# A float32 mixture of 32 experts beside a context stream: fewer turns, every second one of three experts

## What is computed

```python
def routed_moe(h, w_router, b_router, w1, b1, w2, b2):     # h: 256 tokens x 1024, 32 experts
    logits = (xt @ w_router + b_router).astype(jnp.float32)
    top_v, top_e = lax.top_k(logits, 4)
    gates = jax.nn.softmax(top_v, axis=-1)
    ...
    def expert_block(args):                                # w1[e]: 1024 x 2048, w2[e]: 1024 x 1024
        xb, e = args
        return clamped_swiglu(xb @ w1[e] + b1[e]) @ w2[e] + b2[e]
    ...
    y = jnp.zeros((T, D), h.dtype).at[row_tok].add(yb * row_gate[:, None].astype(yb.dtype))

# second block, first layer, for the context rows: retention, then a squared-ReLU MLP
yc = finish(o_cf + flip(o_cb), g_c)
ctx = layer_norm(DN_ALPHA * ctx + g1c * yc, ln_g[i, 0], ln_b[i, 0])
ctx = layer_norm(DN_ALPHA * ctx + g2c * sq_relu_mlp(hc, mlp_w1[i], mlp_w2[i]), ln_g[i, 1], ln_b[i, 1])
```

## Time and profile before

| | before |
|---|---|
| median of 3 runs | 2652.26 us (2649.83 to 2655.31) |
| profiled execution | 2649.32 us, span 2647.5 us |
| TensorE busy | 2388.3 us (90% of the span) |
| VectorE / ScalarE / POOL busy | 55% / 24% / 4% |
| moved by DMA | 711.89 MB, mean 269 GB/s |
| granted TensorE clock, mean | 0.967 of full |

### The profile page before, as it was taken

The page is one execution under the profiler, slowest core; times in us unless marked ns, Lnnn a source line. Parts: engine busy times, 40 slices in busy tenths (PEclk is TensorE's granted clock), DMA queues, the critical chain, the costliest instruction groups (busy, mean ns, idle before and its releaser), DMA issues.

```text
span 2647.5 us, 43597 instructions
## 1 busy us (share of the span) xinstructions
PE 2388.3 (90%) x18084; PEld 1596.5 (60%) x18084; DVE 1448.4 (55%) x2805; ACT 633.9 (24%) x795; POOL 111.1 (4%) x195
## 2 busy tenths in 40 slices
PE   6998988999999899888889898899998999996998
PEld 5887633444444453345445454477767987774897
DVE  2446445444343343555444444576668766776876
ACT  1111211122121121111111111133443433332432
POOL 0000010000000000000000000000000000000000
PEclk8999999999999999999999999999999999998999
DMA  8788888988999799888989888543435542322652
GB/s 345 297 309 328 325 349 328 363 351 349 390 361 368 301 376 373 346 309 324 364 311 365 324 351 319 220 167 139 155 127 207 190 143 98 110 98 88 221 185 77
DMA packets 111249, 711.89 MB, mean 269 GB/s; under 512 B 12480, under 2 KB 13136, under 8 KB 36128
## 3 DMA queue, kind: packets, MB, share of 16 engines
q1 hardware_dynamic: 85904, 616.93, 60.1%
q0 software_dynamic: 25168, 92.38, 9.8%
HBM read 705.06 MB, written 4.19 MB: 268 GB/s over the span
## 4 chain that ended last, share of the span: by engine, by line
PE 74%; DVE 19%; issue 3%; ACT 3%; DMA 1%; DVEq 0%; SPq 0%; ACTq 0%
PE bank L269 25%; PE bank L2176 6%; PE bank L2157 5%; PE bank L1894 5%; PE bank L1932 4%; PE bank L1909 3%; PE bank L1559 3%; PE bank L1416 2%; PE bank L2042 2%; DMA ring<-in_units_a 1%; PE bank L2261 1%; PE bank L1818 1%; PE bank L2031 1%; PE bank L2073 1%; DVE scratch L2938 1%
## 5 line engine op out<-in xcount | busy, mean ns | idle before, releaser
L269 PE MATMUL bank<-hid,scratch 128*32 128x512 f32 x816 | 339.3, 595 | 0.0
L269 PE MATMUL bank<-hT,scratch 128*32 128x512 f32 x784 | 336.3, 597 | 0.0
L1188 ACT CAST chi<-craw 128x1024 fp32r<-128x1024 f32 x128 | 133.3, 1043 | 581.2 <-PE bank L1894 172.4
L3158 DVE TENSOR_TENSOR clo<-craw,chi 128x1024 fp32r<-128x1024 f32 x128 | 155.6, 1221 | 41.7 <-ACT chi L1188 41.0
L269 PE MATMUL bank<-yacc,scratch 128*32 128x512 f32 x1128 | 175.1, 597 | 0.0
L269 PE MATMUL bank<-diag_gtmp,scratch 128*32 128x512 f32 x1128 | 173.2, 592 | 0.0
L269 PE MATMUL bank<-rows,scratch 128*32 128x512 f32 x1112 | 172.5, 600 | 0.0
L269 PE MATMUL bank<-cst,scratch 128*32 128x512 f32 x1112 | 170.4, 593 | 0.0
L1894 PE MATMUL bank<-cT_hi,chi 128*128 128x256 f32 x384 | 116.6, 304 | 40.2 <-DVE crot_lo L3132 17.2
L2948 DVE TENSOR_SCALAR scratch<-bank 128x512 f32<-128x512 f32 x32 | 22.1, 692 | 217.9 <-PE bank L269 217.9
L2944 DVE TENSOR_SCALAR scratch<-bank 128x512 f32<-128x512 f32 x32 | 22.1, 692 | 210.0 <-PE bank L269 210.0
(11 more groups left out here) (664 smaller groups left out, 6045.5 us busy)
## 6 DMA issues: line engine op xcount, KB each, us to landing
hid<-in_panels_e SPq DMA_DIRECT2D x96, 1024.0 KB, 9.9
hT<-in_panels_e SPq DMA_DIRECT2D x94, 1024.0 KB, 9.8
ring<-in_units_a SPq DMA_DIRECT2D x88, 1024.0 KB, 7.3
ring<-in_panels_m SPq DMA_DIRECT2D x64, 1024.0 KB, 5.1
yacc<-in_panels_e SPq DMA_DIRECT2D x48, 1024.0 KB, 6.7
diag_gtmp<-in_panels_e SPq DMA_DIRECT2D x48, 1024.0 KB, 8.8
rows<-in_panels_e SPq DMA_DIRECT2D x47, 1024.0 KB, 7.2
cst<-in_panels_e SPq DMA_DIRECT2D x47, 1024.0 KB, 8.3
```

The lines of the kernel that those rows point to most:

```text
L269: m = self.pe.matmul(b[s:s + STRIP, :], lhs(k)[:, s:s + STRIP], v, start=(first and k == 0), stop=(k == KT - 1))
L1188: act.copy(chi[:, h % 2, :], context_raw(h)).then_inc(cx_hi, 1)
L3158: tt(context_lower(h), context_raw(h), chi[:, h % 2, :], ALU.subtract).then_inc(cx_lo, 1)
```

## The change

The 12 turns after the start turn have, in alternation, two experts (96 and 32 slots) and three (64, 32 and 32 slots). Six turns of two and six of three hold the other 30 experts, so that there are 13 turns where there were 16. By the sorting the 6 fullest experts get 96 slots, the next 6 get 64, the other 18 get 32. The order of loads becomes: for each half of a panel, one load for each expert of the turn. The eight places are handed round load by load (`place_of(m) = (m - 4) % 8`) and no longer by panel, and a load waits for the half panel that used its place eight loads before (`user_before`). SP's loop over turns is written out. TensorE's wait is for all halves of a half panel at its start. The context stream has 12 points in a turn, so one lies in the middle of each panel too; points of a turn of three get 5 shares of the pieces, points of a turn of two 2. The further turns load one panel half for both experts, and there may be 18.

```diff
-TURNS = (32 - STATIC) // 2
+SHARES = ((MANY, SLOTS - MANY), (64, 32, 32)) * 6
+TURNS = len(SHARES)
-POINTS = 6
+POINTS = 12
+HELD = 12
...
+STEPS = [(panel, h) for panel, shares in ((6 * (turn + 1) + j, shares) for turn, shares in enumerate((FIRST_SHARES,) + SHARES, -1)
+                                          for j in range(6)) for h in range(2) for _ in shares]
+def place_of(m):
+    return m if m < HELD else (m - 4) % 8
+def user_before(m):
+    return STEPS[m - 12 if m < 20 else m - 8]
...
+    share = [5 if len(SHARES[n // POINTS]) == 3 else 2 for n in range(number - 1)]
+    ends = [sum(share[:n + 1]) for n in range(number - 1)]
     for n in range(len(pieces) - 2):
-        at[n * number // (len(pieces) - 2)].append(n)
+        at[next(k for k, end in enumerate(ends) if n * ends[-1] < end * (len(pieces) - 2))].append(n)
...
+    def rows(self, b, lhs, first, h):
+        panels = self.halves(h)
+        for k in range(4 * h, 4 * h + 4):
+            for n, s in enumerate(range(0, SLOTS, STRIP)):
+                v = panels[self.owner[n]][:, k % 4, :]
                 m = self.pe.matmul(b[s:s + STRIP, :], lhs(k)[:, s:s + STRIP], v, start=(first and k == 0), stop=(k == KT - 1))
...
+            def next_half(src, m, h):
+                panel, half = user_before(m)
+                if released[half] < panel + 1:
+                    sp.wait_ge((E["half0"], E["done"])[half], panel + 1)
+                    released[half] = panel + 1
+                half_panel(src, m, h)
...
-            with turns(sp, TURNS, {loads: 6}) as i:
-                both = [sp.value_load(order_e[0:1, bass.ds(i * 2 + p, 1)], min_val=0, max_val=EXPERTS - 1) for p in range(2)]
+            for turn, shares in enumerate(SHARES):
+                who = [sp.value_load(order_e[0:1, first_of(turn) + p:first_of(turn) + p + 1], min_val=0, max_val=EXPERTS - 1)
+                       for p in range(len(shares))]
                 for j in range(6):
-                    panels_of_two([at(pe_, e * 6 + j) for e in both], loads)
+                    for h in range(2):
+                        for p, e in enumerate(who):
+                            next_half(at(pe_, e * 6 + j), load_of(turn, j, h) + p, h)
...
-                first_product(0, many)
+                first_product(0, lambda: beside(0))
...
-                beside(0)
-                first_product(1, many)
+                beside(1)
+                first_product(1, lambda: beside(2))
```

## The result

The changed kernel takes 2447.91 us in the median of 4 runs (2444.53 to 2454.49), against 2651.91 us before. The ratio is 0.9233, with an interval of 0.9209 to 0.9256: 204 us or 7.7% faster. Its profiled execution took 2445.24 us, span 2443.5.

A forecast was written before the change was run, and what follows sets the result against it. TensorE was taken to set the pace, with the loads following. From 2649.3 us, -151 for three turns, +24 and +3 for losses to loads and -6 for context waits gave 2519, stated as 2520 us, range 2475 to 2570.

The forecast's parts named there:

- the sum's 2519: Whole kernel: the profiled execution's 2649.3 us with all terms added, 2649.3 - 151 + 24 + 3 - 6.
- What set the pace before: Expert turns of the kernel before: TensorE sets the pace, its waits name only VectorE's tiles, and the loads follow.
- Three turns fewer, -151 us: Expert turns on TensorE: each turn dropped saves 50.4 us of matmuls, gather, transposes and combine, 151 us for three.
- The context's own waits, -6 us with -25 as its bound: TensorE waiting for context pieces in the turns: 6 us less, bounds 0 and 25, though proportion gave 39.
- The one wait on which I leaned, 2.7 us: Context stream before the change: a matmul at 567.78 waits 2.7 us for clo where two pieces stand together.
- The clock, taken as no gain: TensorE in the turns: half-speed stretches after waits; one more per turn of three would cost 10 us, inside the 24.
- The loss of turns of three, +24 and +3 us: Expert turns: TensorE and full DMA engines sharing eight places lose 4 us a turn of three, 0.5 a turn of two.
- TensorE stays alone and the context waits shrink: Rival for the expert turns: no loss to loads, 25 us of waits gone, 2476 us; chance 15%.
- the ceiling of 363 GB/s: Rival for the loads: DMA engines can't hold 407 GB/s for long; 363 as limit gives 2595 us; chance 5%.
- The rival was to decide at 19.5 us: Landing time of panel loads: 19.5 us as usual value decides; at 21 us the kernel takes 2705 us; chance 3%.
- The signs: Trace of the turns: alternately near 77 and 117 us, 1160 to 1175 together, tens of us of panel waits, DMA share 0.97.
- the second rival: Expert turns: TensorE never waits for a panel and context waits shrink by 25 us, 2476 us; chance 15%.

The follow-up runs named there:

- e3: Changed kernel with every panel load after the start turn moving half its bytes, same TensorE instructions: 2436.83 us.
- e1: Changed kernel's 12 turns, but context pieces only at the six points a turn of the kernel before: 2545.55 us, ratio 0.9606 to before.
- e2: Finer context points alone: 15 turns of two experts as before, all else as in the changed kernel: 2535.79 us, ratio 0.9556 to before.
- e8: Changed kernel with the second context piece of a point moved two depths into the following half panel on TensorE: 2436.74 us.
- e5: Changed kernel with equal shares of context pieces for every turn instead of 5 to 2: 2475.31 us.
- e6: Changed kernel with six places for half panels instead of eight: 2494.90 us.
- e13: The changed kernel itself again, five executions on one chip as reference: 2447.13 us, ratio 0.9222 to before.

## Why the prediction was right or wrong

The prediction had the right bound and the right main term, and missed by 72 us, above all because it sized the second half of the change at almost nothing. From the sum's 2519 to the profiled execution's 2445 it is 74 us: 45 are the context's waits, 20.5 the waits for panels, 11 TensorE's busy time with the gather, and 3 us outside the turns go the other way.

**What set the pace before: right.** TensorE did, and it still does (e3). One reading was loose: TensorE's list before is not VectorE's alone, 0.7 us in it is for a tile of ScalarE.

**Three turns fewer, -151 us: right in size.** e1 against before gives 143.7 us of busy time and 2.8 of the gather's wait less, at 14 us more of lost clock in the turns. The changed kernel against e2 gives 144.1 and 4.3 less, at 15 more. So a turn costs 49 us as it stands; I had 50.4. At full clock it would be 53 to 55, an estimate that still holds the cuts that go with a turn: the context stands at 146 places in e2 and at 114 in the changed kernel, at 90 before and at 72 in e1.

**The context's own waits, -6 us with -25 as its bound: this is the step that failed.** Measured are 103.6 - 52.4 = 51 us. The count of second pieces, 56 before and 32 after, was in the prediction with its proportional result of 39 us, and was then talked down: the cover between pieces would be a half panel instead of a whole one, and time won on TensorE would be lost to the loads. Neither discount held (the second comes true only one step further on, in e8). e2 has half a panel between single pieces and 9.7 us of waits, so there 3.6 us of cover is nearly always enough. Divided evenly, the waits are 1.9 us a second piece before, 1.4 in e1, 1.6 in the changed kernel. But they are not all of this kind: with the 12 new turns, 3 second pieces (e5) leave 22.4 us, and from there to the 74 of e1 each adds about 1.1 us. From e2 to before it is 1.7. The one wait on which I leaned, 2.7 us, was a short one. Here is the longest of the changed kernel, in order of time:

```profile
692.45 1.04 PE L1984 MATMUL bank<-cst,cg 128*128 128x128 f32 x8
699.78 0.80 PE L1992 MATMUL bank<-chi,crot_hi 128*128 128x512 f32 x1 [6.29 <-DVE crot_lo L3192]
700.38 0.63 PE L1992 MATMUL bank<-clo,crot_hi 128*128 128x512 f32 x1
700.80 0.63 PE L1992 MATMUL bank<-chi,crot_lo 128*128 128x512 f32 x1
```

The matmul waits 6.3 us for crot_lo, which VectorE splits off from the product before it, and the matmuls that follow run at half the clock for over 3 us (0.63 us each, 0.42 apart).

**The clock, taken as no gain: it was one.** I only asked whether new waits would add half-speed stretches. With fewer waits there are fewer of them: lost clock in the turns is 36 us before and 15 in the changed kernel, 20 us that stand in no term of the sum (16 if only TensorE's busy time counts). The Trainium skill (TensorE: Matmul & The Clock Gate, HAM oscillation — how this bites in real kernels) tells of a kernel that is throttled again at each wait for a DMA. Here the waits are for VectorE, and the traces agree with its picture: e1, with 103 us of context waits, has the granted clock at 0.96 in its turns, and e2, with 9.7, at 1.00 and no half-speed stretch.

**The loss of turns of three, +24 and +3 us: the mechanism is real, the size was that of another kernel.** Waits for panels are 6.5 us. With context only between whole panels (e1) they are 24.7, close to the 27 of the prediction; with six places for eight (e6) they are 50. That the points do this is shown; that they do it by spacing the demand for loads is my reading. I had not connected the two parts of the change.

**What I had left out: the cost of the finer points.** With single pieces in the middle of panels, something costs TensorE about 21 us in e2, most likely the changes between expert and context matmuls. It is as large as the 20 us of the clock, so that the two hid each other in the busy time.

The sum by measurement, for the turns: -159.5 of busy time at full clock (three turns, changed kernel against e2), -20.5 clock (changed kernel against before), +21.4 for cutting the panels (e2 against before), -3.7 gather, -51.2 context waits, +6.5 panels: -207.0, as in the windows. It comes out by its making, for the first three are one difference of busy time, -158.6, taken apart; how it divides into the three rests on the clock.

**The rivals.** "TensorE stays alone and the context waits shrink" was the nearest, with 15% and 2476 us; it too stopped at 25 us of waits and left the clock out. The DMA engines did hold their rate: 120 us at 418 GB/s, above the 407 of the sum, so the ceiling of 363 GB/s did not hold. The Trainium skill (DMA: Bandwidth & Descriptors, Specifications) gives about 358 GB/s for one core, as half of a stack's 716; this core, in a kernel that runs on one core, moved more:

```profile
1310.00:1430.00 120.00, 114.65 (x853) 61.83 (x852) 61.82 (x112) 20.52 (x23) 7.94 (x15) 0.99 1.02 418
```

Landing times did grow, from 8.8 to 11.4 us in the median and from 17.1 to 22.2 at worst. The rival was to decide at 19.5 us as the usual value, and the usual value stayed far under it:

```profile
DMA to landing us min/median/max: 4.9/11.4/22.2
```

It didn't slow the kernel: waits for panels are 6.5 us, and half the bytes (e3) win 3 us in the turns. That the longer landings are loads issued behind others is the reason I had given; it was not tested.

**The signs.** The DMA share came as named (1.00 at 408 GB/s over all the turns). The turns together take 1084 us and not 1160 to 1175, the waits for panels are 6.5 us and not tens, and SP's wait for places keeps its share of the turns. By my own words the near absence of waits for panels points at the second rival. From comb to comb the turns were not near 77 and 117 either: they alternate between 64 to 88 and 94 to 102 us. The comb tile is written late in a turn, so the stretch between two holds part of the context of both; I had not thought of it. This sign could not have tested the 50.4 us; e1 and e2 do.

**What stays open.** The split between clock and cutting cost (20 and 21 us) rests on the assumption that lost clock is lost time, also where TensorE waits; without it they are 16 and 14. Lost clock also varies between executions: the changed kernel's turns lose 15 us in one and 20.5 in another (e13). The cutting cost has no run of its own. Over the span e8 loses 66 us of clock, 54 of them outside its turns, where the changed kernel loses 48; its turns have six half-speed stretches where the changed kernel's have eight. What sets off those that stay was not followed up.

## What to carry to other kernels

When a filler stream is cut finer and spread, count how many of its pieces directly follow another. Here the waits grew with that number, by 1.1 to 1.7 us for each, on top of 10 to 26 us that stayed without any; with half as much other work between single pieces as before, few waits were left. Add the clock that the waits take, and what the cuts cost. And test a change of two parts as two: the finer points alone were worth 116 us, the fewer turns alone 106, and together they made 204.

## What the runs showed of the hardware

- The DMA engines moved 408 GB/s over 1084 us and 418 over 120 us on this one core, and TensorE waited 6.5 us for them. A DMA share of 1.00 and a TensorE that sets the pace can stand together: half the bytes changed the turns by 3 us.
- Over the 1183 us of e2's turns, in which no wait of TensorE is longer than 2.3 us, its granted clock was 1.00; in e1, with context waits of up to 8.1 us, it was 0.96. In the turns that is 50 us more of lost clock.
- The same 5760 expert matmuls were busy for 651.6 us in e2, at a granted clock of 1.00, and for 642.3 us before, at 0.97. In e2 the context stands between them at 75 places inside panels, before at 15.
